# Gate parts stored to DRAM in four pieces of 32 keys, each issued behind the copy of a following gate chunk

## The reference, cut to what matters

```python
def peer_ffn(h, w_query, sub_keys, u_tab, v_tab):
    q = (h @ w_query).reshape(B, L, PEER_HEADS, 2, PEER_QDIM // 2)
    s = jnp.einsum('blhtd,htnd->blhtn', q, sub_keys).astype(F32)
    s1, i1 = lax.top_k(s[..., 0, :], PEER_TOPK)
    s2, i2 = lax.top_k(s[..., 1, :], PEER_TOPK)
    ...
    idx = jnp.take_along_axis(cidx, pos, axis=-1)
    g = jax.nn.softmax(top, axis=-1).astype(h.dtype)
    ...
        act = jax.nn.gelu(jnp.einsum('td,tkd->tk', hx, u_tab[ix]))
        return jnp.einsum('tk,tkd->td', gx * act, v_tab[ix])
```

## Time and profile before

| | us |
|---|---|
| median of 3 runs | 3198.16 (3197.5 to 3198.71) |
| the profiled execution, its own time | 3196.52 |
| its span, first to last instruction | 3194.7 |
| TensorE busy in the span | 2976.4 (93%) |
| VectorE busy | 2033.5 (64%) |
| ScalarE busy | 1257.6 (39%) |
| gates part of the first mixer, from the first chunk to the end of product 39 | about 518 to 678 |
| the same of the second mixer | about 2116 to 2275 |

### The profile page before, as it was taken

The page is one execution under the profiler, slowest core; times in us unless marked ns, Lnnn a source line. Parts: engine busy times, 40 slices in busy tenths (PEclk is TensorE's granted clock), DMA queues, the critical chain, the costliest instruction groups (busy, mean ns, idle before and its releaser), DMA issues. The chain is left out here.

```text
span 3194.7 us, 48644 instructions
## 1 busy us (share of the span) xinstructions
PE 2976.4 (93%) x17528; PEld 2678.2 (84%) x17528; DVE 2033.5 (64%) x4004; ACT 1257.6 (39%) x1826; POOL 128.3 (4%) x100
## 2 busy tenths in 40 slices
PE   7967898899999999999898888988999999999997
PEld 4946798889999999988687787988899999999885
DVE  8877689864348998878736655899544344344454
ACT  3343445753333333333342234447533333333332
POOL 0000250000000000000000002500000000000000
PEclk9988899999999999999888888999999999999998
DMA  5712243664447777767612232435744444544563
GB/s 209 277 52 103 80 138 132 231 251 155 155 143 264 258 249 250 241 201 223 198 62 100 76 120 80 138 132 231 264 145 152 156 146 151 156 147 150 152 177 105
DMA packets 325055, 531.15 MB, mean 166 GB/s; under 512 B 215600, under 2 KB 218416, under 8 KB 319936
## 3 DMA queue, kind: packets, MB, share of 16 engines
q1 hardware_dynamic: 322048, 479.18, 46.3%
q10 hardware_dynamic: 2880, 50.33, 3.9%
HBM read 452.14 MB, written 77.30 MB: 166 GB/s over the span
## 5 line engine op out<-in xcount | busy, mean ns | idle before, releaser
L1967 PE MATMUL pe_s<-peer_hi,pq_uh 128*128 128x384 f32 x2304 | 788.5, 342 | 25.8 <-DVE peer_lo L163 12.6
L1969 PE MATMUL pe_s<-peer_hi,pq_ul 128*128 128x384 f32 x2304 | 777.5, 337 | 0.0
L1968 PE MATMUL pe_s<-peer_lo,pq_uh 128*128 128x384 f32 x2304 | 777.4, 337 | 0.0
L163 DVE TENSOR_TENSOR val_vl<-val_vr,val_vh 128x1024 fp32r<-128x1024 f32 x256 | 313.7, 1225 | 705.3 <-ACT val_vh L2131 705.1
L2067 ACT ACTIVATE pe_A<-pe_s 128x384 f32 (+1 forms) x256 | 126.8, 495 | 1032.6 <-PE pe_s L1969 1031.6
L1967 PEld LDWEIGHTS pe_s<-peer_hi,pq_uh 128*128 128x128 f32 x2304 | 438.3, 190 | 46.0 <-issue 25.6
L2034 PE MATMUL peer_acc<-val_vh,val_wh 128*128 128x512 f32 x1536 | 473.4, 389 | 0.7 <-DVE val_wl L163 0.7
L2034 PE MATMUL peer_acc<-val_vh,val_wl 128*128 128x512 f32 x1536 | 474.0, 390 | 0.0
L2034 PE MATMUL peer_acc<-val_vl,val_wh 128*128 128x512 f32 x1536 | 472.9, 389 | 0.0
L1968 PEld LDWEIGHTS pe_s<-peer_lo,pq_uh 128*128 128x128 f32 x2304 | 438.7, 190 | 7.8
L1969 PEld LDWEIGHTS pe_s<-peer_hi,pq_ul 128*128 128x128 f32 x2304 | 437.7, 190 | 0.0
(11 more groups left out here) (457 smaller groups left out, 3462.7 us busy)
## 6 DMA issues: line engine op xcount, KB each, us to landing
pq_ur<-in_peer_u SPq DMA_DIRECT2D x256, 512.0 KB, 3.7
val_vr<-in_peer_v SPq DMA_DIRECT2D x256, 512.0 KB, 4.4
val_gr<-gates SPq DMA_DIRECT2D x256, 192.0 KB, 4.5
val_mrow<-in_ada_rows SPq DMA_DIRECT2D x56, 512.0 KB, 4.5
gates<-gate_stg ACTq DMA_DIRECT2D x6, 4096.0 KB, 14.2
pq_ur<-in_w_query SPq DMA_DIRECT2D x32, 512.0 KB, 3.6
s_wv<-val_out SPq DMA_DIRECT2D x32, 512.0 KB, 5.3
gates<-gate_stg ACTq DMA_DIRECT2D x4, 3072.0 KB, 12.9
```

Source lines behind the costliest of these rows:

```text
L163: return nc.vector.tensor_tensor(r32(out), x, hi, ALU.subtract)
L1967: pe.matmul(o, r32(uh[:, b, k]), r32(hi[:, k]), start=k == 0, stop=False)
L1968: pe.matmul(o, r32(uh[:, b, k]), r32(lo[:, k]), start=False, stop=False)
L1969: mm = pe.matmul(o, r32(ul[:, b, k]), r32(hi[:, k]), start=False, stop=k == KC - 1)
```

## The change

A part is no longer stored at once when it is full. It is cut into PIECES = 4 pieces of 32 keys, 1 MB each (8 KB in each partition). The first is issued, as before, behind a wait for the copy of the part's last chunk. The others are issued behind the copies of the next three chunks, which go into the other half of `stg`; they have no wait of their own. The pieces count on the semaphores as the stores did, and the waits count four pieces for an even part and three for the rest of an odd one. The two late stores of part 5 stay as they are. No computation is changed, and no table load, copy or matmul is added or moved in an engine's order.

```diff
@@ sync
                 if n == RING - 2:
-                    sp.wait_ge(gst0, 16 * NT)
+                    sp.wait_ge(gst0, 16 * PIECES * NT)
@@ sync, value loop
-                        sp.wait_ge(gst2, 16 * (NT + 1))
+                        sp.wait_ge(gst2, 16 * ((PIECES - 1) * (NT - 1) + 2))
@@ scalar, gates(c)
                 if at == 0 and part >= 2:
-                    act.wait_ge((gst0, gst1)[half], part // 2 * 16)
-                    if half:
-                        act.wait_ge(gst2, part // 2 * 16)
+                    if half == 0:
+                        act.wait_ge(gst0, part // 2 * 16 * PIECES)
+                    else:
+                        act.wait_ge(gst1, part // 2 * 16)
+                        act.wait_ge(gst2, part // 2 * 16 * (PIECES - 1))
...
-                if at + CT == HALF:
+                full = HALF // CT - 1
+                if c >= full:
+                    store_piece(c, (c - full) // (full + 1), (c - full) % (full + 1))
+
+            def store_piece(c, part, k):
+                if k == 0:
                     act.wait_ge(evacd, c + 1)
-                    dst = gates_dram[part]
-                    if half == 0:
-                        act.dma_start(dst, stg[:, 0]).then_inc(gst0, 16)
-                    else:
-                        act.dma_start(dst[:, 0:SOON], stg[:, 1, 0:SOON]).then_inc(gst1, 16)
-                        if part < 2 * NT - 1:
-                            store_rest(part, SOON, NKEYS)
+                half, keys = part % 2, slice(k * SOON, (k + 1) * SOON)
+                if half == 0 and k < PIECES:
+                    act.dma_start(gates_dram[part][:, keys], stg[:, 0, keys]).then_inc(gst0, 16)
+                elif half == 1 and k == 0:
+                    act.dma_start(gates_dram[part][:, keys], stg[:, 1, keys]).then_inc(gst1, 16)
+                elif half == 1 and k < PIECES:
+                    act.dma_start(gates_dram[part][:, keys], stg[:, 1, keys]).then_inc(gst2, 16)
```

More of the change, by code:

```diff
@@ L1687 @@
 REST = (NKEYS - SOON) // 2
+PIECES = NKEYS // SOON
 def slots(eng, emit, looped=True):
```

## The result

| | before | after |
|---|---|---|
| median in us | 3198.43 (3197.5 to 3200.73, 4 runs) | 3165.59 (3162.58 to 3170.47, 4 runs) |
| ratio of the two | | 0.9901, 95% interval 0.9885 to 0.9916 |
| profiled execution, its own time | 3196.52 | 3165.88 |
| its span | 3194.7 | 3164.1 |

The change takes 1% off, 32.8 us in these runs, between 27 and 37 by the interval. The direction was forecast, and so was the way it comes about: tables land earlier, and what ScalarE still waits for them no longer stops TensorE. The size was not: 24.6 us were forecast, and the range ended at 3167, 1.4 us above what came.

What follows compares the result with a forecast made beforehand. Stores were taken to make table loads late, stopping ScalarE and then TensorE. Of 28.3 us lost, 3.7 stay, so 24.6 come off 3196.5, giving 3171.9; plus 1.6 to the median, 3173.5 us, range 3167 to 3188.

Steps and rivals of the forecast that it cites:

- What bounds the kernel: Gates stretches: stores delay table loads, ScalarE waits (26.3 us in the first layer), TensorE stops and its clock drops.
- How much is lost: Both gates stretches against the undisturbed beat: late tables cost 17.0 + 11.3 = 28.3 us, the most to regain.
- Landing of the first table: Table issued 3.5 us into part 0's burst: lands in 6.2 to 7.4 us; ScalarE waits 0.6 to 1.8 us.
- the sum is the same by either rule: Table landing beside pieces: 6.2 us by rows in turn, 6.7 to 7.4 by plain order, giving the same total.
- The term of 3.7 us for waits that add up: Gates stretches: one place in each layer where table waits still stop TensorE, 1.85 us each, 3.7 us charged.
- The bound of 2.8 us: ScalarE's table waits in the gates stretches: waits up to some 2.8 us cost TensorE nothing.
- The range: Whole kernel: 3167 to 3188 us, from all of the 28.3 us and a little over regained to 10 us less.
- ScalarE's queue: Thirteen more store issues a layer on ScalarE, 0.34 to 0.39 us each, taken to cost nothing.
- Waits whose count changed: Waits for pieces before ScalarE's copies and SyncE's first value loads: cost nothing, SyncE's margin 1 to 2 us.
- Half of it: Tables in the ten bursts still land 3 to 4 us late, about 3184 us; chance 0.25.
- No change: Store queue goes ahead of the table queue whatever is in it, 3196 to 3198 us; chance 0.10.
- Slower: Stores of part of a row are slow, so ScalarE waits to refill halves of the buffer, 3238 us; chance 0.05.

Runs made afterwards that it cites:

- e6: Changed kernel, but each piece stores one key (32 KB) instead of 1 MB and every gate load reads key 0; 3167.56 us.
- e9: Changed kernel with two 2 MB pieces of 16 KB rows instead of four, the second issued two chunks later; 3182.44 us, ratio 0.9951 to the kernel before.
- e7: Changed kernel with each piece made of every fourth partition, rows of 32 KB, issues spread as there; 3181.24 us, ratio 0.9936 to the kernel before.
- e1: Changed kernel with all four 1 MB pieces (8 KB rows) issued at once, where the whole store was; 3181.13 us, ratio 0.995 to the kernel before.
- e8: Changed kernel with pieces of every fourth partition, rows of 32 KB, all four issued at once; 3201.4 us, ratio 1.0014 to the kernel before.
- e2: Changed kernel with pieces of 32 neighbouring partitions, rows of 32 KB, issues spread as there; 3281.23 us.
- e3: Changed kernel with pieces of 32 neighbouring partitions, rows of 32 KB, all four issued at once; 3280.91 us.

## Why the prediction was right and wrong

**What bounds the kernel: right.** Late tables stopped ScalarE, then TensorE, then lowered its clock. In the profile after, the waits that are left are within the slack, no copy is late and the clock stays up, and e6 shows that nothing else of the stores was on the path.

**How much is lost: the method was right, the size a little low.** 28.3 us were read from one execution. In the traces of before and after, the two stretches lost 169.0 + 165.1 - 152.0 - 153.8 = 28.3 us, to the tenth what the prediction called the most that could come back. The second pair of profiles has 168.6 + 166.8 - 152.0 - 152.2 = 31.2 us. So the ceiling was one draw of something that varies by 3 us.

**Landing of the first table: right, for half of the reason.** 6.2 to 7.4 us were given, and 6.8 came at this place (6.6 to 8.0 over the five bursts). ScalarE was to wait 0.6 to 1.8 us and waited 1.23. There was luck in it: the third piece was issued 0.04 us ahead of the table and not 0.6 us behind, and with just such a near tie the table lands in 9.7 us in e9 and in anything from 5.4 to 8.8 in e7. Here exactly 2 MB had moved when the table's first row came, and 0.8 MB of the later pieces passed beside it. But the sentence that the sum is the same by either rule was wrong. Each rule alone describes a kernel (e1, e7) that gains half. By plain order the rows of 32 KB would have done as well, and e7 shows that they don't on the mean. By the Trainium skill's rule of turns at packet granularity (DMA: Bandwidth & Descriptors, "Queues, rings and completion order"), with a row for a packet as the prediction took it (the page itself counts some 9 to 17 descriptors to a packet), the 8 KB rows issued at once would have landed the table in 6.2 us, and in e1 it took 10.1. From the table's first row on the traces agree with turns, 32 rows against 32; they don't for the 4.7 us ahead of it. So it is chance that nine times 512 KB, 11.4 us, came near the 11.3 us of before: there the table stood for 4.8 us, and 96 of its 128 rows moved behind the start of the store's last row. The measurements decide: both issue time and row size count.

**The term of 3.7 us for waits that add up: wrong.** This is the step of the sum that failed. It was taken from the place of the earlier trace rows, where 3.33 us of waiting were put at 1.85. In the changed kernel the longest wait for a table is 2.7 us:

```profile
ACT pq_uh L2054 <- DMA pq_ur<-in_peer_u: 7.9, 6, 2.7
```

This is the second stretch; its 153.8 us are the undisturbed 152.0 and the 1.8 of the slot ahead of the first store, so TensorE lost nothing to these waits. In the second profile one is 2.8 us long, and the stretch takes 152.2. The bound of 2.8 us that the earlier trace rows gave was to be trusted: the term measured 0. The price was high as well: it put the lower clock at 0.7 of the stop, and over both layers it was 0.45 (8.7 us against 19.5). Without it the sum is 28.3 us less and 3169.8 us, inside the range and still 4.2 above what came.

**The range: wrong at its lower end.** It ended 31 us below the runs of before, "all of the 28.3 us and a little over", and the medians are 32.8 us apart. The 7.9 us from 3173.5 down to 3165.6 can be placed by the two profiles: 3.7 are the term above; 2.3 lie outside the two stretches, where the executions scatter; and 1.9 are the step from the profiled execution to the median, which was taken as 1.6 us up and was 0.3 down in the changed kernel. Neither this scatter, 3 to 5 us in each of the two parts of the span outside the stretches, nor the 3 us by which the loss itself differs between executions was in the range. The change is worth 31.0 us in one pair of measurements and 32.8 in the other; 28 to 31 of them can be placed in the stretches.

**ScalarE's queue: right.** Issues beside running instructions cost nothing; no activations stand apart except behind the first piece, 0.47 us. What I hadn't seen is that this holds only because they are spread: four in a row cost 3.25 us (e1).

**Waits whose count changed: right.** No wait for a store stands ahead of a gate copy. SyncE issued the first value loads of the first layer at 656.70, 18.2 us after the first piece of part 4, where 17.4 had been worked out; the last piece had landed at 652.9. The margin was 3.8 us, wider than the 1 to 2 given. Behind them it does wait, 1.6 us for the first 1 MB of part 5 ahead of the first gates, where before it was 0.5 us. I had not named that one. The slots behind it take 4.16 us each, the time of a bare product, so it delays nothing.

**The rivals.** "Half of it" is what the incomplete forms of the change do (e1, e7, e9, all 3181 to 3182 us). "No change" is nearest to e8, which is 6 us slower than before; its reason, that the store queue goes ahead whatever is in it, holds only until the table's first row. "Slower" came true for pieces cut by neighbouring partitions (e2, e3), with a burst of 23.3 us. Its price, 40 us, was too low by half, since I had priced the buffers alone: here no copy waits for a half, and it is the late tables that cost 86 us.

## What to carry to other kernels

A large store on one queue can make short loads on another queue late, even when the store's queue has 3.9% of the transfer engines' time. Find it by the load's time to landing and not by the queue's share, and cut the store both in time and in row length; in these runs rows of 8 KB were short enough. Count the packets of each queue in a window to see whether the load stands or shares. A wait that an engine can absorb is free up to its slack, so read the slack from waits that are already in the trace, and then trust it. When all of a loss is expected back, the range must reach past it by what the loss and the rest of the span scatter between executions.

## What the runs showed of the hardware

- A store of 1 MB from 32 neighbouring partitions, with nothing ahead of it, takes 6.6 us to land (e2), from every fourth partition, with the same row length, 4.2 us (e7), and from all 128 with rows of 8 KB 3.9 us.
- An issue of a transfer takes ScalarE's queue 0.34 to 0.45 us in the kernel before and up to 0.83 us in the changed kernel; beside a running activation it costs nothing. Four in a row take 3.2 us with rows of 8 KB (e1) and 4.0 us with 32 rows of 32 KB each (e8).
- A 512 KB load of 4 KB rows that is issued 1 to 4 us behind a 4 MB store on the other queue moves nothing for 4.5 to 4.8 us; with 1 MB pieces spread over some 4 us it is 1.9 to 2.7 us, and with next to no store traffic 1.0 us (e6). Then rows of both queues move about one for one.
- With 32 KB rows issued over some 4 us on the other queue the landing of this load scatters from 5.4 to 13.4 us (e7, both layers); with 8 KB or 4 KB rows it is 6.3 to 8.3 us over all profiles. Beside a second store of 2 MB it is 9.7 us where that is issued 0.03 us ahead of the load, 11.4 us where it is issued 0.86 us behind and the load waits 5.1 us for its first row, and 5.6 us where it is issued 0.33 us behind and the load waits 1.7 us (e9).
- The same slot of work took TensorE 8.78 us at a mean granted clock of 0.84 and 7.09 us at 1.00.
